# Expert weights as sixteen-kilobyte rows, with the second norm and the gated activation written in a permuted order

## What is computed

```python
def _modulate(x, g, shift, scale):
    return _rmsnorm(x, g) * (1 + scale) + shift
...
def _moe(h, w_router, router_bias, w_gate, w_up, w_down):
    shp = h.shape
    hf = h.reshape(-1, shp[-1])
    combine = _route(hf, w_router, router_bias).astype(h.dtype)
    y = jnp.zeros_like(hf)
    for e in range(N_EXPERTS):
        a = jax.nn.silu(hf @ w_gate[e]) * (hf @ w_up[e])
        y = y + combine[:, e:e + 1] * (a @ w_down[e])
    return y.reshape(shp)
```

## Time and profile before

| | |
|---|---|
| three timed runs | 2110.77 us median, 2109.45 to 2118.57 |
| span of the profiled execution | 2108.4 us |
| TensorE (PE) busy | 2012.3 us, 95% of the span |
| VectorE (DVE) busy | 495.8 us, 24% |
| ScalarE (ACT) busy | 368.3 us, 17% |
| hardware queue q1 | 142784 packets, 322.97 MB |
| software queue q0 | 17056 packets, 58.00 MB |
| w_e_gate, w_e_up, w_e_down loads | 32 each, 2 MB each |

### The profile page before, as it was taken

The page is one execution under the profiler, slowest core; times in us unless marked ns, Lnnn a source line. Parts: engine busy times, 40 slices in busy tenths (PEclk is TensorE's granted clock), DMA queues, the critical chain, the costliest instruction groups (busy, mean ns, idle before and its releaser), DMA issues. The chain is left out here.

```text
span 2108.4 us, 16774 instructions
## 1 busy us (share of the span) xinstructions
PE 2012.3 (95%) x6259; PEld 943.3 (45%) x6259; DVE 495.8 (24%) x1256; ACT 368.3 (17%) x797; POOL 123.5 (6%) x186
## 2 busy tenths in 40 slices
PE   7999999999999999999999999999999969999992
PEld 1244445564444444344444424445644434444441
DVE  0332035651011134101010155125501220101002
ACT  1011035551000110010010012125500110101001
POOL 1100000010000000100000020000200000000001
PEclk9999999999999998999999999999999969999996
DMA  9932210011113036999999794220143279999962
GB/s 333 381 140 80 80 51 1 6 26 60 69 51 120 18 133 247 326 342 327 344 327 339 261 336 169 80 90 1 36 141 113 81 272 350 324 340 340 327 216 90
DMA packets 178038, 388.43 MB, mean 184 GB/s; under 512 B 22834, under 2 KB 26962, under 8 KB 177964
## 3 DMA queue, kind: packets, MB, share of 16 engines
q1 hardware_dynamic: 142784, 322.97, 43.1%
q0 software_dynamic: 17056, 58.00, 7.2%
q10 hardware_dynamic: 18132, 6.58, 1.2%
HBM read 366.45 MB, written 21.07 MB: 184 GB/s over the span
## 5 line engine op out<-in xcount | busy, mean ns | idle before, releaser
L1464 PE MATMUL bank<-ring_sb,QR_sb 128*128 128x512 f32 x1024 | 447.6, 595 | 3.5 <-ACT QR_sb L765 3.5
L1464 PEld LDWEIGHTS bank<-ring_sb,QR_sb 128*128 128x128 f32 x1024 | 193.3, 191 | 235.3 <-issue 230.7
L1309 PE MATMUL bank<-ring_sb,HT_sb 128*128 128x512 f32 x672 | 295.9, 596 | 2.7 <-ACT HT_sb L614 1.5
L1375 PE MATMUL bank<-ring_sb,HT_sb 128*128 128x512 f32 x576 | 253.3, 593 | 1.4 <-ACT QR_sb L731 1.4
L1475 PE MATMUL bank<-ring_sb,QR_sb 128*128 128x512 f32 x512 | 225.2, 593 | 1.7 <-issue 1.7
L1309 PEld LDWEIGHTS bank<-ring_sb,HT_sb 128*128 128x128 f32 x672 | 126.0, 191 | 149.4 <-issue 147.4
L1375 PEld LDWEIGHTS bank<-ring_sb,HT_sb 128*128 128x128 f32 x576 | 109.5, 190 | 138.5 <-issue 136.6
L1260 PE MATMUL bank<-ring_sb,cT_sb 128*2 128x512 f32 x384 | 170.0, 603 | 1.4 <-DMA ring_sb<-w_mod 1.4
L1475 PEld LDWEIGHTS bank<-ring_sb,QR_sb 128*128 128x128 f32 x512 | 95.1, 190 | 110.0 <-issue 110.0
L1337 PE MATMUL bank<-KR_sb,QR_sb 64*128 64x512 f32 (+1 forms) x288 | 141.4, 575 | 1.6 <-ACT QR_sb L649 1.6
L1364 PE MATMUL bank<-WK_sb,KR_sb 128*64 128x128 f32 x960 | 136.9, 283 | 0.0
(11 more groups left out here) (177 smaller groups left out, 1192.0 us busy)
## 6 DMA issues: line engine op xcount, KB each, us to landing
ring_sb<-w_e_gate SPq DMA_DIRECT2D x32, 2048.0 KB, 9.5
ring_sb<-w_e_up SPq DMA_DIRECT2D x32, 2048.0 KB, 8.8
ring_sb<-w_e_down SPq DMA_DIRECT2D x32, 2048.0 KB, 10.0
ring_sb<-w_mod SPq DMA_DIRECT2D x24, 2048.0 KB, 12.0
ring_sb<-w_in SPq DMA_DIRECT2D x22, 2048.0 KB, 13.7
y_d<-KR_sb POOLq DMA_DIRECT2D x32, 512.0 KB, 8.5
ring_sb<-w_branch SPq DMA_DIRECT2D x6, 2048.0 KB, 7.6
MB_sb<-mod_d POOLq DMA_DIRECT2D x16, 512.0 KB, 8.0
```

Source lines behind the costliest of these rows:

```text
L1309: ins = mm(bank[j % 4][:, :], HT[:, k, P * t:P * t + P], WR[slot][:, k], start=(k == 0), stop=(k == KD - 1))
L1375: ins = mm(bank[i % 2][:, :], HT[:, k, P * t:P * t + P], WR[wg][:, k], start=(k == 0), stop=(k == KD - 1))
L1464: ins = mm(bank[j][:, :], hgT[parity][:, c8], WR[s][:, c8], start=(c8 == 0), stop=(c8 == KD - 1))
```

## The change

The rows of each expert weight are dealt to the partitions in another way. Partition p now holds the neighbouring rows 8p to 8p + 7 of w_gate and w_up (4p to 4p + 3 of w_down), which lie as one run of 16 KB in HBM. Block k then contracts over the rows 8q + k, so the activation's column 8q + k has to come out on partition q of block k. The transposes stay as they are; instead VectorE writes `hn` with column 8q + k of the norm at place 128k + q, and `ea` likewise with four blocks. The router's weights are loaded in the same order, since it reads the same `hn`. The first norm and the final norm keep their order, and so do all other weights.

```diff
             def expert_source(l, e, j):
                 w = t_in[("w_e_gate", "w_e_up", "w_e_down")[j]]
                 w = w[l, e] if isinstance(e, int) else w[l, bass.ds(e, 1)].rearrange("o k n -> (o k) n")
-                return w.rearrange("(k p) n -> p k n", p=P)
+                return w.rearrange("(p k) n -> p k n", p=P)
...
-            dma(wr[:, :, :], t_in["w_router"].rearrange("(k p) e -> p k e", p=P)).then_inc(const_in, 16)
+            dma(wr[:, :, :], t_in["w_router"].rearrange("(p k) e -> p k e", p=P)).then_inc(const_in, 16)
...
-            def modulated(t):
+            def modulated(t, blocked=True):
...
-                link(stt(hn[t % 2], X[:, t], rstd[:, t:t + 1], modb[:, s, 0], ALU.mult, ALU.mult))
-                tt(hn[t % 2], hn[t % 2], modb[:, s, 1], ALU.add).then_inc(hn_ready, 1)
+                made, scale, shift = hn[t % 2], modb[:, s, 0], modb[:, s, 1]
+                if blocked:
+                    link(stt(made, X[:, t], rstd[:, t:t + 1], scale, ALU.mult, ALU.mult))
+                else:
+                    link(stt(made.rearrange("p (k q) -> p q k", k=KD), X[:, t].rearrange("p (q k) -> p q k", k=KD),
+                             rstd[:, t:t + 1], scale.rearrange("p (q k) -> p q k", k=KD), ALU.mult, ALU.mult))
+                    made = made.rearrange("p (k q) -> p k q", k=KD)
+                    shift = shift.rearrange("p (q k) -> p k q", k=KD)
+                tt(made, made, shift, ALU.add).then_inc(hn_ready, 1)
...
-                        modulated(t)
+                        modulated(t, blocked=False)
...
-                    tt(ea, esg, bank[1][:, :], ALU.mult).then_inc(ea_ready, 1)
+                    tt(ea.rearrange("p (k q) -> p q k", k=4), esg.rearrange("p (q k) -> p q k", k=4),
+                       bank[1][:, :].rearrange("p (q k) -> p q k", k=4), ALU.mult).then_inc(ea_ready, 1)
```

More of the change, by code:

```diff
@@ L1174, in _ @@
                             eng.wait_ge(q["silu"], n + 1)
-                            tt(ea, esg, bank[1][:, :], ALU.mult).then_inc(q["a"], 1)
+                            tt(ea.rearrange("p (k q) -> p q k", k=4), esg.rearrange("p (q k) -> p q k", k=4),
+                               bank[1][:, :].rearrange("p (q k) -> p q k", k=4), ALU.mult).then_inc(q["a"], 1)
                             eng.wait_ge(q["a_tr"], n + 1)
```

## The result

The changed kernel is slower: 2131.79 us (median of 4 runs, 2123.92 to 2133.12) against 2110.55 for the kernel before, with a fourth run beside its three (2109.45 to 2118.57), a ratio of 1.0083 with a 95% interval of 1.0054 to 1.0111. The profiled execution is the quickest of the four, with a span of 2122.2 us, 13.8 over the one before.

The account below looks back on a forecast made before the run. TensorE's own instructions were taken to bound the kernel (busy 2012.3 of 2108.4 us). Loads 0, shared engines 0, second norm 0.5 and gated activation 0 gave 0.5 us on the median of 2110.77: 2111.3 us, range 2107 to 2148.

Parts of the forecast that it names:

- What bounds the kernel: In the expert loop, TensorE's own instructions set the 21.9 us an expert; no expert weight is waited for.
- The gather's margin: Next expert's gather lands 8.9 to 9.2 us after issue, needed at 11.9: 2.7 to 3.0 us spare in every steady-loop expert.
- The first rival: Next expert's gather becomes TensorE's wait at the transposes, from a landing of 11.9 us: 34 us, 2145 us; chance 0.30.
- the 24 gathers: Gathers for experts 3 to 14, 12 a layer, with the store ahead and a gate load coming.
- part 2: Store and gather sharing DMA engines with the weight loads: no wait, 0 us; bounds 0 and 2.8 us an expert.
- the walk: One DMA engine followed through one expert: gather lands at 965.6, before 965.92; fast row 963.8, slow row 968.7.
- The rival's price: Gather waits at TensorE's transposes: 1.4 us each, half the upper bound, at 24 gathers, 34 us; chance 0.30.
- The one-for-one turns: On the DMA engines, two queues alternate packets whatever their size; a 16 KB row between gather rows takes 0.64 to 0.75 us.
- The norm: Second norm's two hopping VectorE instructions: 1.15 us longer a tile, 0.5 us on the path in layer 2 (0 to 1.6).
- The gated activation: VectorE's hopping write in each of 32: 0.3 us longer (0 to 0.6), covered by down, so 0.
- The router's weights: Their load: 1,024 packets fewer, less 128, far from any wait, so 0.
- The faster rival: At the change of layers, traffic clears sooner: 3 us gained, 2108 us; chance 0.07, of which 0.02 over 0.5%.

Follow-up runs that it names:

- vector_only: The changed kernel with expert weights loaded as before, so only VectorE's writes and the router weights are permuted: 2114.94 us, ratio 1.0008 to the kernel before.

## Why the prediction was wrong in its forecast and right in its rival

- **What bounds the kernel, and that no weight is waited for**: right. TensorE's list after has no expert weight.
- **The gather's margin of 2.7 to 3.0 us**: right for the stretch that was read, and it is where the loss is. It did not hold "in every expert": in the second layer one gather before (issued at 1976.64) took 10.4 us, 1.5 us ahead of the deadline. The first rival named the place (L1239, now L1248), the deadline (a landing of 11.9 us) and the 24 gathers. I gave it 0.30 and forecast no wait. The measured ratio has its lower end above 1.005. The measured 2131.79 us misses the forecast's own range (2107 to 2116) and lies in the whole range (2107 to 2148) only because that took in this rival.
- **The step that failed** is the end of part 2: "I take no wait as the value", a term of 0. One walk through one engine gave one landing for all gathers, 11.5 us after issue, and was then read as all or none. Its own midpoint, 966.2, lay behind the deadline of 965.92 and was still priced at nothing. In the profile the typical gather lands at 9.5 us, sooner than the walk, and a fifth to two fifths of the 24 land at 12.3 to 15.8; one in each execution is past the walk's slow bound (968.7 - 954.05 = 14.6). It is the spread that the long rows raised: the median by 0.6 us, the slowest by 6.5. Measured: 5 and 9 waits for a gather in the two profiled executions of the changed kernel, 8.0 and 14.0 us of waiting in all, and 11.0 us over both layers' experts in the first, the fall of the clock included.
- **The rival's price** has the same flaw: 1.4 us at every one of 24 gathers, 34 us. A late gather cost 1.6 us of waiting in the mean, but only 5 or 9 were late. That 1.4 is so near is luck, since it was half of a bound.
- **A choice in the walk that was off**: a load's first row 1.5 us after issue. In the late expert the software queue is nearly alone until 984, 2.3 us after the gate load's issue at 981.63. By the walk's 0.16 us a row, 0.8 us more are five small rows, the five that it had left over. That fits with most gathers being in time; no run tests it alone.
- **The one-for-one turns** were read from too little. The earlier trace rows counts the packets of 16 engines in one microsecond, so it shows neither the order on one engine nor a turn "whatever their size". The trickle in the late expert fits such turns with 16 KB rows, but no view shows one engine's queue.
- **The price of a wait**: I counted the wait alone. The fall of the granted clock after an idle stretch was missing from the term: at the 3.73 us wait it added 2.7. The other four waits, of 0.4 to 1.7 us, brought no such fall: the eight transposes behind each took 1.09 us, as against 1.97 behind the long one.
- **The norm**: the size was off. The last tile in layer 2, first a row of before beside the earlier trace rows, then the changed kernel, then vector_only:

```profile
1683.81 1.28 DVE L864 SCALAR_TENSOR_TENSOR WK_sb<-X_sb,rstd_sb,MB_sb 128x1024 f32<-128x1024 f32 x1
...
1695.66 1.99 DVE L868 SCALAR_TENSOR_TENSOR WK_sb<-X_sb,rstd_sb,MB_sb 128x1024 f32<-128x1024 f32 x1
...
1696.55 3.27 PE L1403 MATMUL bank<-wr_sb,HT_sb 128*128 128x16 f32 x16 [3.21 <-ACT HT_sb L614]
1697.69 2.04 DVE L872 TENSOR_TENSOR WK_sb<-WK_sb,MB_sb 128x1024 f32<-128x1024 f32 x1
1699.79 1.12 PE L1248 MATMUL bank<-tab_sb,WK_sb 128*128 128x128 f32 x4
...
1692.68 2.11 PE L1403 MATMUL bank<-wr_sb,HT_sb 128*128 128x16 f32 x16 [3.21 <-ACT HT_sb L614]
1695.90 1.97 PE L1248 MATMUL bank<-tab_sb,WK_sb 128*128 128x128 f32 x8 [1.11 <-DVE WK_sb L872]
```

  The two are 0.71 and 0.82 us longer than the 1.28 and 1.22 us of before, 1.53 for my 1.15. From the reciprocal that precedes them (1683.61 before, 1695.46 now) to the transposes it is 4.33 us for 3.43, so 0.9 us show for my 0.5. In the changed kernel's profile the router's matmuls (L1403) also end only then: they take 3.27 us, most of it at a granted clock of 0.50. In vector_only they take 2.11 us, TensorE waits 1.11 us for VectorE, and the stretch is 4.31 us all the same (1691.59 to 1695.90), so it is the norm that sets it. The two differences are 0.69 and 0.80 ns an element; 16 elements were too few to read 0.56 from. The Trainium skill, "Vector Engine (DVE) Microarchitecture Reference", section 5.2, has 1.71 ns a column for an output that hops 4 KB with every element, 0.66 more than contiguous, and the first instruction's 0.69 agrees with it, at a hop of 512 bytes. The prediction's estimate from these figures, 1.3 to 2.8 us for a tile, takes in the measured 1.53; its upper end is an error of the sum, since one instruction at 2.50 and one at 1.73 give 2.2 us.
- **The gated activation**: 1053 ns for 687, 0.37 us for my 0.3, and hidden by down as forecast. At the first expert of each layer TensorE waits 0.32 us for it, and the time from that gate to the next stays 16.05 us in the first layer.
- **The router's weights**: 896 packets fewer were expected. The software queue, which loads them, has 17056 packets before and after, so nothing of it shows.
- **The faster rival**: nothing of it shows. The wait for VectorE at the change of layers is 2.4 us for 2.5.

## What to carry to other kernels

Before lengthening the rows of a bulk transfer, look for the small transfer with the nearest deadline on the same engines, and compare its slowest landing, not its median, with its slack. If two queues take turns row by row, which fits the traces here but is not shown by them, a long row of one is a long wait for each short row of the other. If the bulk transfer is never waited for, as here, a sooner landing gains nothing, and longer rows can only cost. If they are wanted, issue the small transfer first or a turn sooner.

## What the runs showed of the hardware

- Halving the number of the loads' packets left their landing time where it was: 9.3, 9.1 and 9.8 us for 9.5, 8.8 and 10.0. In this kernel 2 KB rows were already as good as 16 KB ones.
- A gather of 128 rows of 4 KB behind a store of as many goes from 9.2 us at worst to 15.8 when the loads' rows are 16 KB, and from 11.1 to 18.0 with a second store ahead (both for gathers issued from 905 to 1190 us). In that second pair, from 1000 to 1100 us, the share of the DMA engines in use is 0.97 with short rows and 0.67 with long ones.
- Long rows in down alone, or in gate and up alone, gave no late gather; why down's long rows alone spread it to 11.4 us while the amount of data stays the same, the runs do not show. Nor do they show which engine is the last.
